# Upward strips of two MLPs with high and low activations as one 512-column operand, on one Trainium2 core

## What is computed

```python
a = jnp.square(jax.nn.relu(rms_norm(h, g_mlp[l]) @ w_up[l]))
h = h + a @ w_down[l]
...
proj = h @ w_in[i]
...
mixed = jax.nn.sigmoid(g_ma) * (y_a @ w_o_a[i]) + jax.nn.sigmoid(g_mb) * (y_b @ w_o_b[i])
x = x + mixed @ w_out[i]
h2 = _rmsnorm(x, norm2_g[i])
x = x + jnp.square(jax.nn.relu(h2 @ w_up[i])) @ w_down[i]
```

## Time and profile before

| | |
|---|---|
| median of 3 runs | 880.17 us |
| profiled execution, time | 880.41 us |
| profiled execution, span of its instructions | 878.6 us |
| PE busy | 869.0 us, 99% of the span |
| POOL busy | 680.8 us, 77% |
| DVE busy | 453.7 us, 52% |
| ACT busy | 429.6 us, 49% |
| chain that ended last | PE 85%, DVE 10%, ACT 2% |

### The profile page before, as it was taken

The page is one execution under the profiler, slowest core; times in us unless marked ns, Lnnn a source line. Parts: engine busy times, 40 slices in busy tenths (PEclk is TensorE's granted clock), DMA queues, the critical chain, the costliest instruction groups (busy, mean ns, idle before and its releaser), DMA issues.

```text
span 878.6 us, 13266 instructions
## 1 busy us (share of the span) xinstructions
PE 869.0 (99%) x5362; PEld 754.1 (86%) x5362; DVE 453.7 (52%) x659; ACT 429.6 (49%) x590; POOL 680.8 (77%) x387
## 2 busy tenths in 40 slices
PE   9999999999999999999999999999999999999998
PEld 7898977898899999998887788777778899999996
DVE  5697652423453222325698799559934551223333
ACT  6674486365353443443853655546445454434330
POOL 3789583958679999988997879803527889999881
PEclk9999999999999999999999999999999999999999
DMA  9865442624445665655845444610223546656531
GB/s 336 340 211 196 147 163 96 214 98 153 159 168 194 210 216 193 200 185 163 312 144 167 139 158 144 215 49 2 97 97 126 164 152 215 206 195 210 196 115 48
DMA packets 65554, 149.22 MB, mean 170 GB/s; under 512 B 4800, under 2 KB 9952, under 8 KB 65376
## 3 DMA queue, kind: packets, MB, share of 16 engines
q1 hardware_dynamic: 65504, 148.53, 50.1%
HBM read 147.47 MB, written 1.05 MB: 169 GB/s over the span
## 4 chain that ended last, share of the span: by engine, by line
PE 85%; DVE 10%; ACT 2%; issue 1%; POOL 1%; DMA 1%; ACTq 0%; DVEq 0%
PE ps L1866 73%; PE ps L2047 2%; PE ps L2021 2%; PE ps L2089 1%; PE ps L1959 1%; PE ps L2033 1%; PE ps L1852 1%; PE ps L2294 1%; DVE xn L1558 1%; DVE xn L1758 1%; DVE arena L1318 1%; PE ps L2212 1%; PE ps L2233 1%; DVE arena L1560 1%; POOL w_lo L672 1%
## 5 line engine op out<-in xcount | busy, mean ns | idle before, releaser
L672 POOL TENSOR_TENSOR w_lo<-raw,w_hi 128x512 fp32r<-128x512 f32 (+2 forms) x362 | 668.9, 1887 | 143.6 <-ACT w_hi L715 143.4
L715 ACT ACTIVATE w_hi<-raw 128x1024 fp32r<-128x1024 f32 (+2 forms) x193 | 247.7, 1321 | 250.2 <-PE ps L1866 121.1
L1866 PE MATMUL ps<-w_hi,x_hi 128*128 128x512 f32 (+1 forms) x672 | 267.6, 398 | 2.0 <-DVE x_lo L1121 2.0
L1866 PE MATMUL ps<-w_hi,x_lo 128*128 128x512 f32 (+1 forms) x672 | 260.8, 388 | 0.0
L1866 PE MATMUL ps<-w_lo,x_hi 128*128 128x512 f32 (+1 forms) x672 | 260.6, 388 | 0.0
L1866 PE MATMUL ps<-x_hi,w_hi 128*128 128x256 f32 x704 | 201.6, 286 | 0.0
L1866 PE MATMUL ps<-x_hi,w_lo 128*128 128x256 f32 x704 | 199.2, 283 | 0.0
L1866 PE MATMUL ps<-x_lo,w_hi 128*128 128x256 f32 x704 | 199.1, 283 | 0.0
L1866 PEld LDWEIGHTS ps<-w_hi,x_hi 128*128 128x128 f32 x672 | 126.7, 188 | 33.5 <-issue 8.6
L1866 PEld LDWEIGHTS ps<-w_hi,x_lo 128*128 128x128 f32 x672 | 126.5, 188 | 26.6
L1866 PEld LDWEIGHTS ps<-w_lo,x_hi 128*128 128x128 f32 x672 | 126.8, 189 | 23.1
(11 more groups left out here) (285 smaller groups left out, 815.0 us busy)
## 6 DMA issues: line engine op xcount, KB each, us to landing
raw<-in_w_in SPq DMA_DIRECT2D x33, 1024.0 KB, 5.3
raw<-in_w_up SPq DMA_DIRECT2D x32, 1024.0 KB, 5.4
raw<-in_w_down SPq DMA_DIRECT2D x32, 1024.0 KB, 4.8
raw<-in_w_xkv SPq DMA_DIRECT2D x8, 1024.0 KB, 5.0
raw<-in_w_out SPq DMA_DIRECT2D x8, 1024.0 KB, 4.8
raw<-in_w_xq SPq DMA_DIRECT2D x4, 1024.0 KB, 5.0
raw<-in_w_xo SPq DMA_DIRECT2D x4, 1024.0 KB, 4.9
raw<-in_w_in SPq DMA_DIRECT2D x6, 512.0 KB, 8.1
```

What stands on the lines that cost most here:

```text
L672: x = nc.gpsimd.tensor_tensor(LO[s % 2][:, 2048 * q + d0:2048 * q + d1], RAW[n % 3][:, d0:d1], HI[s % 2][:, 2048 * q + d0:2048 * q + d1].b ...
L715: nc.scalar.activation(HI[s % 2][:, 2048 * q + c0:2048 * q + c1], RAW[n % 3][:, c0:c1], ACT.Copy).then_inc(hi_done, 1)
L1866: last = T.matmul(dst, l, r, start=start and i == 0, stop=stop and i == 2, skip_group_check=w_stationary)
```

## The change

Three edits.

1. **Up strips j >= 2** of both MLPs. High and low activations get one buffer `XX` each, so that a matmul can move 256 high and 256 low columns as one operand. A step is two matmuls: w_hi with both (512 columns, a whole bank for each o), and w_lo with the high part. The two halves of a bank have to be added afterwards, by ACT (copy of the second half), and DVE (`activate_wide`). All four banks 4 to 7 are used by each such strip, so that it waits for `a_lo` of the strip before. The factor is taken as its square, `rB2`, made at the start of each MLP. In the diff, `mlp` with `before` is ACT's, the one without it DVE's.
2. **Columns of `w_in_2`**: strips IN2+7 and IN2+8 get 338 columns each.
3. **End of the units**: strip IN2+12 ends one hook earlier (k = 26); the two fill blocks come in the hook of k = 27, in banks 0 and 1; ACT fills before it scales strip 12; DVE takes its parts of the fill in the unit loop.

```diff
+        XX = [sb(f"x_hilo{i}", [P, 4096], f32r) for i in range(2)]
+        XH = [x[:, 0:2048] for x in XX]
+        XL = [x[:, 2048:4096] for x in XX]
...
+        rB2 = diag
...
+        U2_COLS = [512 * c for c in range(8)] + [(3584 + GM) // 2, GM]
...
+            if TB_Y2 <= n < TB_Y2 + 2:
+                return n - TB_Y2
...
             def mlp(base, a0, abuf, before):
                 for i in range(2, 16):
-                    hi(base + i)
+                    hi(base + i, 0)
+                    for j in range(2, 8):
+                        if up_strip(0, j) == i - 2:
+                            act.wait_ge(strip_done, base + i - 1)
+                            nc.scalar.activation(act_q.rearrange("p (o u) -> p o u", u=S), up_rest,
+                                                 ACT.Copy).then_inc(up_copied, 1)
+                    hi(base + i, 1)
...
+            fill_hi(0, 2)
             u2_scaled(12, gate_cols[3])
-            fill_hi(0, 2)
...
+            def activate_wide(j, done, a0, abuf, i):
...
+                dve.wait_ge(up_copied, at(m, 2))
+                V.tensor_tensor(up_sum, up_sum, aq, ALU.add).then_inc(up_evac, 1)
+                dve.wait_ge(up_evac, at(n, 2))
+                V.scalar_tensor_tensor(aq, up_sum, 0.0, bc(rB2.unsqueeze(1), [P, 4, S]),
+                                       ALU.max, ALU.mult).then_inc(up_scaled, 1)
+                dve.wait_ge(up_scaled, at(m, 2))
+                V.scalar_tensor_tensor(up_sum, up_sum, 0.0, aq, ALU.max, ALU.mult).then_inc(sq_ready, 1)
                 dve.wait_ge(sq_ready, at(n, 2))
                 dve.wait_ge(a_hi, at(n, 2))
+                V.tensor_tensor(XL[abuf][:, c].rearrange("p (o u) -> p o u", u=S), up_sum,
+                                XH[abuf][:, c].bitcast(f32).rearrange("p (o u) -> p o u", u=S),
+                                ALU.subtract).then_inc(a_lo, 1)
...
             def mlp(base, a0, abuf):
+                link(V.tensor_tensor(rB2, rB, rB, ALU.mult))
                 for j in (0, 1):
                     activate(j, up_strip(base, j) + 1, a0, abuf)
...
-                        if d["j"] >= 2 or ups[0] >= 8:
-                            pe.wait_ge(up_evac, at(ups[0] - 1, 2))
+                        if d["j"] >= 2:
+                            pe.wait_ge(a_lo, at(ups[0], 2))
...
+                    elif m == "up" and d["j"] >= 2:
+                        c = 2048 * (k // 4) + w * (k % 4) + P * o
+                        both = XX[d["x"]][:, :].rearrange("p (z k u) -> p z k u", z=2, u=S)[:, :, k, :]
+                        T.matmul(bank(4 + o), hi_[:, c:c + P], both, start=k == 0, stop=k == KT - 1,
+                                 skip_group_check=True)
+                        x = T.matmul(bank(4 + o)[:, 0:S], lo_[:, c:c + P], xh[:, S * k:S * k + S], start=False,
+                                     stop=k == KT - 1, skip_group_check=True)
...
-                elif 13 <= k < 28:
-                    strip(IN2 + 12, 16 * (k - 13) // 15, 16 * (k - 12) // 15)
+                elif 13 <= k < 27:
+                    strip(IN2 + 12, 16 * (k - 13) // 14, 16 * (k - 12) // 14)
+                elif k == 27:
                     fill_block(0)
                     fill_block(1)
```

More of the change, by code:

```diff
@@ L95, in build @@
         LO = [sb(f"w_lo{i}", [P, 4096], f32r) for i in range(2)]
-        XH = [sb(f"x_hi{i}", [P, 2048], f32r) for i in range(2)]
-        XL = [sb(f"x_lo{i}", [P, 2048], f32r) for i in range(2)]
+        XX = [sb(f"x_hilo{i}", [P, 4096], f32r) for i in range(2)]
+        XH = [x[:, 0:2048] for x in XX]
+        XL = [x[:, 2048:4096] for x in XX]
         xn = sb("xn", [P, NT, D])
@@ L921, in mlp @@
                             c = slice(1024 * (j % 2), 1024 * (j % 2) + 1024)
-                            nc.scalar.activation(XH[abuf][:, c], act_q, ACT.Copy).then_inc(a_hi, 1)
+                            src = act_q.rearrange("p (o u) -> p o u", u=S) if j < 2 else up_sum
+                            nc.scalar.activation(XH[abuf][:, c].rearrange("p (o u) -> p o u", u=S), src,
+                                                 ACT.Copy).then_inc(a_hi, 1)
             mlp(MLP1, 0, 0, MLP1)
@@ L1123, in fill_lo_block @@
                 fill[0] += b == 3
-            def fill_lo():
-                for b in range(4):
-                    fill_lo_block(b)
             def tb_take(fn, last=None):
@@ L1459, in _, with activate @@
             broadcast_rstd(3, bank(0))
[L1461 to L1466, removed]
+            def activate(j, done, a0, abuf):
+                dve.wait_ge(strip_done, done)
                 V.scalar_tensor_tensor(act_q.rearrange("p (c u) -> p c u", u=S),
@@ L1470, in activate, with at @@
                 n = a0 + j + 1
+                dve.wait_ge(up_evac, n)
+                V.tensor_tensor(act_q, act_q, act_q, ALU.mult).then_inc(sq_ready, 1)
+                dve.wait_ge(sq_ready, n)
+                dve.wait_ge(a_hi, n)
+                c = slice(1024 * (j % 2), 1024 * (j % 2) + 1024)
+                V.tensor_tensor(XL[abuf][:, c], act_q, XH[abuf][:, c].bitcast(f32), ALU.subtract).then_inc(a_lo, 1)
+                dve.wait_ge(a_lo, n)
+            def activate_wide(j, done, a0, abuf, i):
+                def at(count, per_turn):
+                    return i * per_turn + count
+                n, m = a0 + j + 1, a0 // 8 * 6 + j - 1
+                c = slice(1024 * (j % 2), 1024 * (j % 2) + 1024)
+                aq = act_q.rearrange("p (o u) -> p o u", u=S)
+                dve.wait_ge(up_copied, at(m, 2))
+                V.tensor_tensor(up_sum, up_sum, aq, ALU.add).then_inc(up_evac, 1)
                 dve.wait_ge(up_evac, at(n, 2))
[L1472 removed]
+                V.scalar_tensor_tensor(aq, up_sum, 0.0, bc(rB2.unsqueeze(1), [P, 4, S]),
+                                       ALU.max, ALU.mult).then_inc(up_scaled, 1)
+                dve.wait_ge(up_scaled, at(m, 2))
+                V.scalar_tensor_tensor(up_sum, up_sum, 0.0, aq, ALU.max, ALU.mult).then_inc(sq_ready, 1)
                 dve.wait_ge(sq_ready, at(n, 2))
                 dve.wait_ge(a_hi, at(n, 2))
[L1475 to L1476 removed]
+                V.tensor_tensor(XL[abuf][:, c].rearrange("p (o u) -> p o u", u=S), up_sum,
+                                XH[abuf][:, c].bitcast(f32).rearrange("p (o u) -> p o u", u=S),
+                                ALU.subtract).then_inc(a_lo, 1)
                 dve.wait_ge(a_lo, at(n, 2))
[L1479 to L1480 removed]
             def kc_tables():
@@ L1500, in mlp @@
                     for j in (2, 3):
-                        activate(j, up_strip(base, j) + 1, a0, abuf, i)
+                        activate_wide(j, up_strip(base, j) + 1, a0, abuf, i)
             mlp(MLP1, 0, 0)
@@ L1808, in hook2 @@
                     signal(xn_ready, 1)
+                    fill_lo_block(1)
             def early2(i):
@@ L1812, in early2 @@
                     gate_evac(2)
+                if i == NU:
+                    fill_lo_block(0)
             gate_evac(0)
@@ L1816, in _ @@
             signal(xn_ready, 1)
-            fill_lo()
+            fill_lo_block(2)
+            fill_lo_block(3)
             dve.wait_ge(gates_sig, 2)
@@ L2067, in mlp_products @@
                     return
-                pe.wait_ge(up_evac, 8)
+                pe.wait_ge(a_lo, 8)
                 last_strip(s1 - 1)
```

16 lines of the change are left out of this document (9 added, 7 removed).

## The result

| | before | after |
|---|---|---|
| median | 880.38 us (4 runs, 880.09 to 880.73) | 893.04 us (4 runs, 891.81 to 894.16) |
| after by before | | 1.0129, 95% interval 1.0085 to 1.0173 |
| profiled execution | 880.41 us, span 878.6 | 893.19 us, span 891.4 |

The change makes the kernel slower by 12.7 us. The direction was forecast; the time, 884.0 with a range of 879.5 to 888.5, was not. A later series of six runs of the same kernel on another chip had a median of 887.77 us, so that two questions follow: where +7 us come from, and where 5 more.

The account below looks back on a forecast made before the run. PE, busy 869.0 of 878.6 us, was taken to bound the kernel. The terms -5.1 + 8.5 + 2.8 + 0 - 2.4 = +3.8 on 880.41 gave 884.2, as median 884.0 us; range 879.5 to 888.5.

Parts of the forecast that it names:

- DVE waits for the end of POOL's running one, takes its turn, then POOL goes on: Two-SBUF-source DVE operations and POOL's: they hold each other off for whole operations; a POOL operation takes 3.40 instead of 2.41 us.
- the matmuls: Wide up strips: a step falls from 360 to 346.7 ns, 0.43 us a strip, 12 strips, -5.1 us.
- the clock: Half speed after PE's idle time ahead of d0: +1.4 us in each MLP, +2.8; bounds 0 and 2.8 each.
- the units' end: Strip 13 starts 1.0 us earlier and the clock may hold (-1.4): -2.4 us, bounds 0 and -3.6.
- edit 2: 338-column strips: PE's work falls from 16.2 to 14.8 us, but PE waits for DVE's L1718: 0, bounds -1.4 and +1.
- rB2: Square ahead of activate(0): held by POOL, it delays x_lo and d0 by 4.25 us in each MLP, +8.5 us.
- a square that is not held changes little: MLP start: an unheld square would end at 252.7, and the same queue follow some 0.2 us earlier.
- each matmul costs 13.3 ns over its columns: Up and down strips: 120 and 226.7 ns per matmul against 106.7 and 213.3 ns for the columns alone.
- The evacuation: Behind each wide strip: 7.5 us of ACT and DVE work, covered by a 10.9 us down strip: 0.
- the one fall of before: Ahead of strip 13: after 2.0 us idle, 2.82 us of work ran at half pace, 1.4 us lost.
- The wait of 1.3 us for the shared bank: Units' end: PE, done at 642.7, waits until about 644.0 for DVE to take the first product out.
- the rivals: Clean MLP start 872.7 us (0.12); half, 881.2 or 878.3 (0.10); no matmul saving 889.1 (0.05); wide strips wait, +12 (0.02).

Follow-up runs that it names:

- e3: Before with only the square of rB added ahead of activate(0) in both MLPs, its result unused: 893.03 us (4 runs; 1.0125 of before).
- e1: After with the square of rB moved behind activate(0) and activate(1) in both MLPs: 875.64 us (10 runs; 0.9964 of before).
- e2: After with the square at its place, but made with the broadcast's PSUM bank as one source: 887.18 us (10 runs; 1.0084 of before).
- e9: Kernel of e1 with 512 adjacent (not the right) columns as the wide matmul's operand: 879.08 us (10 runs; 0.9990 of before), third chip.
- e8: Kernel of e1 with a bank's matmuls in the order 512, 512, 256, 256 columns: 873.22 us (4 runs; 0.9916 of before).
- e10: As e8, but four 512-column matmuls and then four of 256: 873.14 us (9 runs; 0.9922 of before), third chip.
- e5: After again, unchanged, on another chip: 887.77 us (6 runs; 1.0094 of before).
- e6: Before with the 338-column strips alone: 879.60 us (12 runs; 0.9989 of before).
- e7: Before with the units' end and last strips reordered alone: 877.33 us (11 runs; 0.9981 of before).
- e4: Before with the wide up strips alone, the square placed behind activate(1): 878.49 us (10 runs; 0.9985 of before).
- e11: Kernel of e8 again, with more runs, on a third chip: 872.81 us (12 runs; 0.9922 of before).

## Why the prediction was right in its direction and wrong in its size

The step that put the time outside the range is "DVE waits for the end of POOL's running one, takes its turn, then POOL goes on": at the fill DVE was passed four times instead, +5.2 us. The rest of the 9.0 us between the forecast +3.8 and the span's +12.8 is the matmuls (+2.8), the clock (+1.5), the units' end (+0.9), less edit 2 (-1.1) and rB2 (-0.3). By term:

- **rB2 (+8.5)**: right. 4.1 us in each MLP, +8.2; each operation of the chain within 0.3 us of its forecast end. e3 shows the loss with the square alone, and in e1, without the square there, it is gone. The forecast had it that a square that is not held changes little: e2 shows that.
- **The matmuls (-5.1)**: mis-sized. The step that failed is "each matmul costs 13.3 ns over its columns", so that one matmul less gives 13.3 ns. With both sizes in turn the wide one costs 23 ns over its columns (236 against 213.3) and the narrow one 10. -2.3 came, between the bounds 0 and -5.1. The Trainium skill's 2.5 ns (TensorE: Matmul & The Clock Gate, "Back-to-back issue gap"), which the page gives for a matmul by itself, would make it 1.0 us by estimate; the measured 7 ns a step lie between 2.5 and 13.3. What stays open is why: not the operand's two pieces (e9), and not the size changes alone (e8, e10).
- **The evacuation (0)**: right, to 0.1 us.
- **The clock (+2.8)**: mis-sized, +4.3 in after (2.6 and 1.7), 1.7 and 2.5 in e3, inside the bounds of 0 to 5.6. The step that failed: taking the one fall of before, 2.8 us of work at half pace, for that of any idle time. Here it was 3.4 us of work (1.7 lost) to 5.6 (2.8 lost, e5).
- **Edit 2 (0)**: -1.1 in after's trace, -1.0 in e6's. The step that failed was that DVE's chain stays where it was while PE comes earlier.
- **The units' end (-2.4)**: -1.5 in after's profile, where the clock fell, and -3.1 in e5's and e7's, where it did not: the forecast -2.4 lies between the two and matches neither. The wait of 1.3 us for the shared bank was right (1.4).
- **Not in the forecast**: DVE passed by POOL, +5.2 us in after's profiled run. The prediction had said that DVE "takes its turn" at POOL's next change, as every held operation in before's trace did; the rivals held no case in which it doesn't. Why POOL went first is open.

With the measured sizes: -2.3 + 8.2 + 4.3 - 1.1 - 1.5 = +7.6, and 5.2 for the fill is 12.8, the span's difference. Without this event after would be at 888, at the edge of the range and where four of e5's runs lie. That the fill's event was in all four of after's first runs is likely from their times, 891.8 to 894.2, and from their mean granted clocks, 0.990 to 0.992, which are those of e5's two long runs; but only one of them left a trace, and why that series had it four times of four and e5 at most twice of six is open.

The Trainium skill's rule that DVE and POOL exclude each other where DVE has two inputs in SBUF (SBUF — State Buffer, "Who interferes with whom") agrees with the traces: L1519 took 1.67 us in after with two such sources and 0.42 in e2 with one in PSUM. Its other half, that the order of issue decides who blocks, does not fit the fill, where DVE came 0.07 us ahead of POOL's next operation and still ended behind four of them.

## What to carry to other kernels

Before an operation is put ahead of a hand-over that has less than a microsecond of slack, write down where POOL stands at each step behind it: in e2 a delay of 0.45 us was enough to lose 3.9 us twice, with 4.2 of clock behind. Put such preparations behind the first hand-over; it cost one moved line to turn +7 into -5 us. And take a forecast's durations from the mix in which they will run: matmuls of one size in a row say little of two sizes in turn.

## What the runs showed that was not expected

- **DVE can be passed over by POOL.** An operation of DVE with two SBUF sources mostly had its turn at POOL's next change; but in e4 it was passed six times (9.20 us), in after four times (5.59 us), and in e1, e2 and e5 once (1.92 us). In after and e4 it ended only when POOL had nothing left. In after, e1, e2 and e5 it had been issued 0.07 to 0.08 us ahead of the change, in e4 0.55 us ahead; and in e9 and e10 the operation of the fill, also 0.07 to 0.08 us ahead, was neither passed nor held (0.69 us). So its moment alone does not decide. Of before's 73 runs beside the experiments 13 lie at 884 us or more; this event fits their time, but none of them was profiled, so that it isn't shown.
- **Long runs come more often with the wide strips.** Of the 100 runs of before, e3, e6 and e7, 16 lie more than 4.5 us above their kernel's lowest; of the 71 runs of e1, e2, e4, e5 and e8 to e11, 24 do. In before, e3, e6 and e7 the fill's operation comes 0.5 us ahead of POOL's change, in the others' traces at most 0.15 us ahead. Whether that is the cause was not tested, so the price of the wide strips may hold a share of these long runs.
- **The clock is not the same for the same idle time.** After 1.41 us at the units' end it fell in the traces of after, e1, e8 and e9 and held in those of e2, e5, e7, e10 and e11; after 2.3 us it fell in before, e3 and e6 and held in e4. After 4.24 us it fell each time, and 1.7 to 2.8 us were lost.
- **A matmul's cost depends on its neighbours.** 256 columns took 120 ns among their like, 117 between wide ones and 115 in pairs; 512 columns 227 in down strips and 229 to 236 in wide up strips.
